# Two gaps in the SBUF layout: the rounded weights start 64 bytes past a 128-byte line

## The reference, cut to what matters

```
x = x + hybrid_mixer(rmsnorm(x), w_in, conv_w, ..., w_out)
x = x + memory_cross_attention(rmsnorm(x), rmsnorm(mem), w_q, w_k, w_v, w_o)
x = x + moe_ffn(rmsnorm(x), 32 experts, top 4, swiglu)     # expert width 1024
x = rmsnorm(x)
for i in range(4):                    # attention kinds: a (differential), b (latent), c (dilated), a
    x = x + attention_i(rms_norm(x))
    x = x + swiglu(rms_norm(x), f_w_gu[i], f_w_out[i])     # FFN width 2816
return rms_norm(x)
```

## Time and profile before

| | |
|---|---|
| launch, median of 3 runs (lowest to highest) | 2556.43 us (2556.01 to 2556.81) |
| span of the profiled execution, first to last instruction | 2554.5 us |
| median less span: what lies around it | 1.9 us |
| PE busy | 2520.4 us, 99% |
| PEld busy | 2028.1 us, 79% |
| DVE busy | 1491.8 us, 58% |
| ACT busy | 1082.1 us, 42% |

### The profile page before, as it was taken

One profiled execution on the slowest core, in us unless ns is written; L12 is line 12 of the kernel. 1 busy time (PEld: TensorE's weight loads), 2 busy tenths in 40 slices (PEclk: granted clock), 3 DMA queues, 4 the chain that ended last, 5 costly groups with the idle time before them and its releaser, 6 DMA issues.

```text
span 2554.5 us, 48583 instructions
## 1 busy us (share of the span) xinstructions
PE 2520.4 (99%) x18788; PEld 2028.1 (79%) x18788; DVE 1491.8 (58%) x2995; ACT 1082.1 (42%) x1903; POOL 0.2 (0%) x4
## 2 busy tenths in 40 slices
PE   8999999999999999999999999999999999999998
PEld 7997555565555555558999988999999999999997
DVE  6763333323333233338877777777776777788776
ACT  5442111112211122116755566555445555567544
POOL 0000000000000000000000000000000000000000
PEclk9999999999999999999999999999999999999999
DMA  6456999999999999995455542555544455544552
GB/s 269 165 204 257 422 428 428 429 428 428 429 427 429 428 427 429 429 426 189 146 176 184 191 141 100 190 176 191 202 170 168 143 182 181 184 170 154 185 183 97
DMA packets 71322, 676.02 MB, mean 265 GB/s; under 512 B 8480, under 2 KB 8736, under 8 KB 15648
## 3 DMA queue, kind: packets, MB, share of 16 engines
q1 hardware_dynamic: 64800, 663.84, 66.6%
q10 hardware_dynamic: 6400, 10.49, 1.1%
HBM read 662.76 MB, written 1.05 MB: 260 GB/s over the span
## 4 chain that ended last, share of the span: by engine, by line
PE 91%; ACT 3%; DVE 3%; issue 1%; ACTq 1%; DMA 0%; DVEq 0%; SPq 0%
PE bank L2880 18%; PE bank_pair L2056 12%; PE bank_pair L2898 9%; PE bank_pair L300 6%; PE bank_pair L2057 6%; PE bank_pair L302 6%; PE bank_pair L301 6%; PE bank_pair L2870 5%; PE bank L300 4%; PE bank L301 4%; PE bank L302 4%; PE bank_pair L2887 2%; PE bank L2944 1%; DVE w_lo L276 1%; PE bank_pair L2944 1%
## 5 line engine op out<-in xcount | busy, mean ns | idle before, releaser
L276 DVE TENSOR_TENSOR w_lo<-ring,w_hi 128x1024 fp32r<-128x1024 f32 (+1 forms) x488 | 581.5, 1216 | 132.9 <-ACT w_hi L269 132.2
L269 ACT ACTIVATE w_hi<-ring 128x1024 fp32r<-128x1024 f32 (+1 forms) x486 | 494.7, 1048 | 230.0 <-PE bank_pair L302 136.2
L2056 PE MATMUL bank_pair<-ht,w_hi 128*128 128x512 f32 x1344 | 476.5, 398 | 0.0
L2057 PE MATMUL bank_pair<-ht,w_lo 128*128 128x256 f32 x1344 | 377.5, 281 | 0.0
L2056 PEld LDWEIGHTS bank_pair<-ht,w_hi 128*128 128x128 f32 x1344 | 252.6, 188 | 60.1
L2057 PEld LDWEIGHTS bank_pair<-ht,w_lo 128*128 128x128 f32 x1344 | 254.0, 189 | 0.0
L3085 DVE TENSOR_SCALAR big<-bank_pair,big 128x64 f32<-128x64 f32 x256 | 60.8, 279 | 330.2 <-PE bank_pair L2887 330.2
L2880 PE MATMUL bank<-ring,big 128*64 128x256 f32 x2048 | 235.2, 382 | 0.1
L2880 PE MATMUL bank<-moe_w,big 128*64 128x256 f32 x2048 | 235.2, 382 | 0.0
L300 PE MATMUL bank_pair<-ht,w_hi 128*128 128x256 f32 x768 | 222.3, 289 | 1.7 <-DVE w_lo L276 1.7
L2972 ACT ACTIVATE big<-bank 128x256 f32<-128x256 f32 x128 | 49.2, 384 | 397.5 <-PE bank L2880 397.5
(11 more groups left out here) (420 smaller groups left out, 4540.8 us busy)
## 6 DMA issues: line engine op xcount, KB each, us to landing
ring<-post SPq DMA_DIRECT2D x213, 1024.0 KB, 4.8
ring<-wgu SPq DMA_DIRECT2D x64, 2048.0 KB, 13.4
moe_w<-wgu SPq DMA_DIRECT2D x64, 2048.0 KB, 15.2
big<-wdn SPq DMA_DIRECT2D x32, 2048.0 KB, 17.4
moe_w<-wdn SPq DMA_DIRECT2D x32, 2048.0 KB, 16.0
ring<-pre SPq DMA_DIRECT2D x27, 1024.0 KB, 4.9
prob<-probt ACTq DMA_DIRECT2D x64, 128.0 KB, 3.5
ring<-post SPq DMA_DIRECT2D x3, 768.0 KB, 4.7
```

Source lines behind the costliest of these rows:

```text
L269: act.activation(w_hi[:, u % SR, cs], ring[:, u % R, cs], ACT.Copy).then_inc(ph.hi, 1)
L276: dve.tensor_tensor(w_lo[:, u % SR, cs], ring[:, u % R, cs], f32(w_hi[:, u % SR, cs]), ALU.subtract).then_inc(ph.lo, 1)
L2056: pe.matmul(o, wh[:, k, cs], both[:, :, k, :], start=(k == 0), stop=False, skip_group_check=True)
L2057: mm = pe.matmul(o[:, 0:S], wl[:, k, cs], ht[:, k, :], start=False, stop=(k == KB - 1), skip_group_check=True)
```

## The change

A helper `next_at(line)` adds an unused tile so that the next tile starts at the byte `line` modulo 128, and it is called three times: for `ht` (which lies there already, and nothing is added), for `w_hi` (a gap of 64 bytes), and for `big` (a gap of 96 bytes).

```diff
+        def next_at(line):
+            gap = (line - -(-nc.sbuf_base // 32) * 32) % 128
+            if gap:
+                sb(f"gap{nc.sbuf_base}", [P, gap // 4])
+
         xt = sb("xt", [P, KB, S])
+        next_at(0)
         ht_at = -(-nc.sbuf_base // 32) * 32
         both = sb("ht", [P, 2, KB, S], F32R)
         ...
         hid_hi = sb("hid_hi", [P, 4, S], F32R)
         hid_lo = sb("hid_lo", [P, 4, S], F32R)
+        next_at(64)
         w_hi = sb("w_hi", [P, SR, UW], F32R)
         w_lo = sb("w_lo", [P, SR, UW], F32R)
         ring = sb("ring", [P, R, UW])
         con = sb("con", [P, CONSTS.shape[1]])
         par = sb("par", [P, NPARAM])
+        next_at(0)
         big_at = -(-nc.sbuf_base // 32) * 32
         big = sb("big", [P, 9 * 2048])
```

## The result

| | before | after |
|---|---|---|
| launch, median (lowest to highest) | 2556.62 us (2556.01 to 2556.96) | 2540.51 us (2539.79 to 2541.0) |
| ratio, 95% interval | | 0.9937 [0.9923, 0.9951] |
| span of the profiled execution | 2554.5 us | 2539.2 us |

The change gains 16.1 us, 0.63%, where 42 were forecast. The time lies in the range that was given (2478 to 2558) and inside the first rival, "64 is no better than 32 and 96" (2530 to 2544). The interval of the ratio leaves out 1, so the kernel is faster.

A forecast was written before the change was run, and what follows sets the result against it. PE's matmul starts were taken to bound the kernel, the layout changing only their pace. Gains of 29.5 + 9.7 + 5.1 + 0.3 = 44.6 us, less 5%, gave 42 us: 2514 us, range 2478 to 2558.

The forecast's parts named there:

- 64 is no better than 32 and 96: Rounded matmuls at distance 64 go at 116.7 to 118.4 ns: 12 to 27 us gained, 2530 to 2544; chance 0.22.
- even curve: Pace over operand distance: 120 ns at 0, 117.5 in the mean at 32 and 96, so 115.0 at 64.
- The term of 29.5 us: Weight pieces with `ht` and `hid`, distance 0 to 64: 5904 matmuls gain 5.0 ns each, between 0 and 53 us.
- The pairs' term: FFN's matmuls of 512 and 256 columns, distance 0 to 64: 1344 pairs from 353.2 to 346 ns, 9.7 us.
- The sub-tiles' term: Sub-tiles of `big` with weight pieces: 1500 matmuls from 118.4 and 192 from 116.7 to 115 ns, 5.1 and 0.3 us.
- Nothing for the experts, the transfers and the plain float32: Plain float32 matmuls of experts and attention were taken to gain nothing; expert still 29.07 us, transfers still 428 GB/s.
- the rival that put a price on them: Expert transfers into slots 64 bytes off a line get slower; at 20% in two slots 57 us lost, 2571; chance 0.07.
- 5% for breaks and waits: Waits where a stage begins and first matmuls don't shrink: 5% off the sum of 44.6 us, leaving 42.
- 64 is like 0: Distance 64 acts like 0, if memory repeats every 64 bytes; sub-tiles lose 3.0 us, 2559; chance 0.17.
- The floor of 111 ns: Lower bound for a rounded matmul of 256 columns, set by the load of 128 columns in line 2870.
- 215 ns for 512 columns: Column time read from experts' line 2898, 430 ns for two instructions; with 111 it gave a pair's floor of 326 ns.
- the second rival: The loss vanishes at distance 64: all floors together give 102 us, 2455; the stretch below 2490 had chance 0.07.

The follow-up runs named there:

- 24 for another: Weight pieces at 96, `hid` at 32, `ht` and `big` at 0, against the kernel before the change: 2532.7 us, ratio 0.9909.
- layouts at 32: The changed kernel with the weight pieces at 32 instead of 64, `big` at 0: 2548.27 us, ratio 0.997 to the kernel before.
- the layout at 96: The changed kernel with the weight pieces at 96 instead of 64, `big` at 0: 2539.22 us, ratio 0.9933 to the kernel before.
- stretches at the end: The changed kernel with test matmuls added behind its last stage, other engines idle; the first such run took 2941.35 us with all the added work.

## Why the prediction was wrong in size and right in direction

**What bounds the kernel** held: PE's starts, at one clock, and the layout changes their distances. The rule that the prediction set against its rows, from the Trainium skill's "TensorE: Matmul & The Clock Gate", part 2, that the next load takes no bandwidth from the running matmul, would have given 0; the runs moved by 16 us for this layout and by 24 for another, with the same instructions. What exactly the two streams share was not shown; at distance 0 the size of the load counts (119.9 against 113.35 ns).

**The step that failed** is the pace of distance 64: "If 0 is one end of an even curve, the other end is as far below 117.5 as 120 is above, 115.0 ns." It has two errors. There is no even curve, as the layouts at 32 (2548.27) and 96 (2539.22) show; and a distance does not have one pace. At 64 it has 113.35 and 117.8, and 115.0 is neither. `ht` got a mixture, 115.9, and `hid` nearly always the slow one, 117.6. The term of 29.5 us measured 19.7.

**The pairs' term** of 9.7 us was -0.7. The prediction took 346 ns from "three times 115" and from the first tile. The first tile showed that a second pattern exists at distance 0; it did not show that distance 64 picks it. At 64 every tile goes at 353.5, the first one too, and 96 is where 346.7 is steady. Its own remark, "the pace has more than one steady pattern at one layout", was the right reading of the earlier trace rows, and then the sum took one pace for each distance all the same.

**The sub-tiles' term** of 5.4 us was 2.3 in the distances, and 2.3 by the runs with and without the gap ahead of `big`: right in sign, under half in size, for the same reason.

**Nothing for the experts, the transfers and the plain float32** held: a round of 29.07 us before and after, and transfers into slots that start 64 bytes off a line land as fast (17.3 us against 17.7). Of the rival that put a price on them nothing was seen. **5% for breaks and waits** was too small: 6.0 us of a gain of 21.3 in the paces.

**The rivals.** "64 is no better than 32 and 96" had the right time, 2530 to 2544, and the wrong mechanism: it put all rounded matmuls between 116.7 and 118.4. They are at 113.4 or 117.8, and the mean falls there. Its 3 to 4.5 us for the pairs are not worked out in the prediction and were not there. "64 is like 0" is excluded by all parts but the pairs, for which it is nearly true. The floor of 111 ns was never reached by a full matmul of 256 columns; the lowest steady step in any run was 113.2. The other floor, 215 ns for 512 columns, was misread. The two instructions of a step in the earlier trace rows don't follow each other. They start 6 to 7 ns apart, each on 64 columns of the array (the form 128*64), and the next two start 0.43 us behind the first:

```profile
508.74 0.60 PE L2898 MATMUL bank_pair<-moe_w,big 128*64 128x512 f32 x2
509.17 0.60 PE L2898 MATMUL bank_pair<-big 128*64 128x512 f32 x2
```

So each of them had 430 ns for its 512 columns, and these rows give no price of 215. The 326 of a pair and the 102 us of the second rival rest on it; the forecast does not.

**A second miss** of the same kind was the layout at 96, 11 us over its expectation: steady paces of stretches at the end were carried into the kernel. For the pairs and the sub-tiles that was right, for `ht` and `hid` it was not.

**What stays open**: why a pattern holds, and what in the entry picks it. Cutting the first matmul shows that the entry decides, behind pairs of one pace; it gives no rule by which the pace could be worked out ahead. A single matmul of 64 or 192 columns changed nothing at the end of the kernel, and cuts of 64 and 192 did inside it. It is also open what takes the 2 ns from 111 to 113.3, since a load of a quarter the size does not give them back.

## What to carry to other kernels

When PE streams and loads all the time, its pace is in the distances between starts and not in busy time or durations, and the places of its two operands within a line of 128 bytes can be worth a per cent: here 0.6% for one pair of gaps and 0.9% for another that leaves PE's instructions alone as well. Sweep the offsets for each kind of pair in the kernel itself, since the best distance for one kind (64 for 256 columns) is not that of another (96 for 512 and 256), and since a pace measured by itself may not be the one that a stretch falls into behind its real neighbours. Two paces at one layout are a sign that the pace belongs to the stretch and not to the layout; then neither an average nor a curve through a few layouts is a forecast.

## What the runs showed of the hardware that was not expected

- Float32r matmuls of 256 columns with full weight loads have steady patterns, 113.3, 116.7, 117.8, 118.3 and 120.0 ns a matmul among them, at the same clock. A pattern mostly lasts until the stream is broken or the shape changes, and at the end of the kernel a single short matmul of 128 columns between changed 117.8 to 113.35, where 16, 64 or 192 columns did not. Cutting the first matmul in two did the same inside it, in 31 of 33 units.
- The dependence on the distance is neither even nor mirrored: about 120, 117, 118.2, 116.7 or 119.1, 113.3, 118.3, 116.7, 116.7 or 118.7 from 0 to 112 bytes in steps of 16, and 119 to 123 at the odd multiples of 8.
- The floor of about 113.3 ns for 256 columns stays with loads of only 32 columns. With full loads, 128 and 192 columns come every 111.6 ns, 320 every 146.6, 384 every 173.5 and 448 every 202 to 207.
- A second load of the same weights in place of a wider matmul is free: three matmuls of 256 at 117.8 against 353.5 for 512 and 256.
- The Trainium skill's "SBUF — State Buffer", who interferes with whom, states that PE waits on no other engine there. The runs here don't test that as a whole. They agree as far as the two paces of distance 64 go, which both came (117.8 and 113.35 ns) with every other engine idle.
